# A two-layer transformer step on one core: the first weight unit of three stages taken in pieces

## The chip, the cores and the metric

The kernel runs on one core of a Trainium2 chip. The metric is the device time in microseconds of one execution. Three runs of the kernel before gave 1477.97, 1479.73 and 1479.81 us; the median is 1479.73 us.

## What is computed

One inference step for 384 tokens of width 1024: 128 prompt tokens and 256 sample tokens. Prompt and sample tokens have modulations of their own (shift, scale, gate, from `c_ctx` and `c`). All is float32.

```
for layer 0 and 1:
    h = x * (1 + scale) + shift            (modulate, per group of tokens)
    layer 0: q, k, v, p = h @ w_in_a ; differential attention and pooling ; @ w_out_a
    layer 1: h @ w_in_c ; two-way mLSTM over chunks ; @ w_out_c
    x = LayerNorm(alpha * x + gate * out)
    h = modulate(x)
    layer 0: SwiGLU with ffn_w_gu, ffn_w_down
    layer 1: router, top 2 of 8 experts, each a SwiGLU
    x = LayerNorm(alpha * x + gate * out)
```

The modulations come from `silu(c) @ ada_w + ada_b`, 12 vectors of 1024, so 12 x 4 MB of weights.

## The kernel before, in words

**Products.** Every dense weight comes in units of 128 x 1024 floats (512 KB) through a ring of six slots: `raw` (as loaded by SyncE, `stream`, L422 to L436), `whi` (ScalarE's copy in the rounded type, `Splits`, L453) and `wlo` (VectorE's remainder, raw minus whi, L456). The activations are held in the same two parts: `H32` is the modulated input, `Hh` its rounded copy, `Hl` the remainder. A product is three matmuls, whi x Hh, whi x Hl and wlo x Hh. `t_product` (L470 to L472) takes a unit of 128 output columns against all 384 tokens: for each of the eight chunks k of 128 channels three matmuls of 384 columns, so 24 matmuls. Its result goes to bank 6 or 7 of PSUM in turn; the semaphores free6 and free7 say when a reader has emptied the bank. Units of `ada_w` are not split; they go through the ring as `raw` and are multiplied with 32 columns of weights (L600).

**The start.** SyncE issues nine small loads (constants, masks, vectors), four units of `ada_w`, the three tiles of X, and then the stream. ScalarE waits for all nine (`cst_loaded`) before it makes the conditioning vectors. PE multiplies four ada units, waits for X, turns X with 24 transposes (L696), and goes on with ada units until the first two modulation vectors are there (`modc_made`; 16 units). With them ScalarE (L717) and VectorE (L729) make H32 out of PSUM, tile by tile of 128 tokens; ScalarE rounds (L745, L751), VectorE subtracts (L757, L760). `hl_made` counts finished tiles. `pe_mixer0` waits for all three and then takes, in the order of `INA_ORDER`, one t-unit of `w_in_a` and two ada units, eight times (they are called t0 to t7 here), and then units of the value part. GpSimd issues the loads of the caches and of the pooling matrices (2 MB) when the second modulation vector is there (`arow_made`).

**Between the stages.** Behind the output projection of layer 0 and behind its SwiGLU a norm follows, written out by hand for each engine (`dve_norm`, `act_norm`, `n_last`, `pe_turn`). They are called norm 0 and norm 1 here. VectorE scales tile t, PE turns it, ScalarE (and for half of the third tile VectorE) modulates it, ScalarE rounds, VectorE subtracts. `keep_clock` (L523) issues matmuls whose result nobody reads, 18 and then 12. When all of Hl is made (`hl_made`), GpSimd multiplies X with the norm's gain and adds its bias in six operations on 128 x 1024 (`pool_norm`, L849 and L850).

**Behind norm 0** `pe_ffn` waits for two tiles, but its first product reads all three and so stands behind the last piece of Hl. The order of units is g0, u0, g1, u1, d0, g2 and on (g and u are t-units, d is of the down projection). VectorE's order there is: split five units (L456), then multiply the first pair (L1227), which frees bank 7, then L1230. u1 writes bank 7, so it needs that first L1227. **Behind norm 1** `pe_mixer1` first makes the gates out of H32 (L1309, 16 matmuls), waits for `hl_made`, and takes 24 t-units m0 to m23. ScalarE copies each out (L1474); between the first and the second copy stands a step on the gates (L1413) that waits for a chain of VectorE (L1426 to L1429), which VectorE starts when it has split three units. m3 needs the bank of m1.

## Time and profile before

| what | value |
|---|---|
| median of three runs | 1479.73 us |
| the profiled execution, its own time | 1475.37 us |
| its span, first to last instruction | 1473.8 us |
| TensorE busy | 1388.6 us, 94% of the span |
| VectorE busy | 896.8 us, 61% |
| ScalarE busy | 725.5 us, 49% |
| GpSimd busy | 217.3 us, 15% |
| mean granted clock of TensorE | 0.979 of full |
| HBM read | 318.12 MB |

TensorE is busy nearly all the time, so a stage's length is mostly its matmuls; where TensorE stands still, the rest of the page says who ended the wait. The profiled execution took 4.4 us less than the median of the runs.

### The profile page before, as it was taken

How to read it: one execution, taken by the hardware profiler on the slowest of the kernel's cores; microseconds unless marked ns; L12 is line 12 of the kernel's file. 1: busy time of each engine (PE TensorE's matmuls, PEld its weight loads, DVE VectorE, ACT ScalarE, POOL GpSimd, SP SyncE). 2: the span in 40 equal slices, each digit the busy share in tenths (PEclk: the TensorE clock that was granted, in tenths of full speed). 3: DMA queues.
4: the chain of work that ended last, by engine and by line, in shares of the span. 5: the costliest groups of instructions: out<-in, count | busy, mean ns of one | idle time of the engine just before them, and what ended most of it. 6: DMA issues, size and time to landing. Idle time of an engine off the chain costs nothing.

```text
span 1473.8 us, 20822 instructions
## 1 busy us (share of the span) xinstructions
PE 1388.6 (94%) x6930; PEld 1142.7 (78%) x6930; DVE 896.8 (61%) x1187; ACT 725.5 (49%) x1125; POOL 217.3 (15%) x278
## 2 busy tenths in 40 slices
PE   6899888999999989999879899999999999999997
PEld 2766467999999979987557788888888888878784
DVE  0425557633333478222886597755555899999997
ACT  1323555232223353322443586445444888888883
POOL 1000001600000014003430372300000520000010
PEclk9999989999999999999999799999999999999998
DMA  9885563784444414537756499866765999999991
GB/s 326 280 266 204 200 197 111 280 288 129 129 129 129 129 43 127 147 113 232 247 195 215 143 345 381 288 186 187 227 187 181 326 383 378 383 372 380 377 364 58
DMA packets 255110, 341.23 MB, mean 232 GB/s; under 512 B 16910, under 2 KB 210732, under 8 KB 254908
## 3 DMA queue, kind: packets, MB, share of 16 engines
q1 hardware_dynamic: 241354, 299.55, 61.8%
q0 software_dynamic: 12400, 40.67, 7.4%
q8 instruction: 45, 0.74, 0.2%
q10 hardware_dynamic: 1282, 0.04, 0.0%
q14 instruction: 29, 0.24, 0.0%
HBM read 318.12 MB, written 21.02 MB: 230 GB/s over the span
## 4 chain that ended last, share of the span: by engine, by line
PE 82%; DVE 10%; ACT 3%; issue 2%; DMA 2%; SPq 1%; DVEq 0%; ACTq 0%
PE PS L2153 25%; PE PS L481 15%; PE PS L2160 12%; PE PS L470 6%; PE PS L471 6%; PE PS L472 6%; PE PS L600 2%; DVE wlo L456 2%; PE PS L2128 1%; PE PS L696 1%; PE PS L625 1%; DMA X<-in_x_sample 1%; DMA raw<-in_w_in_a 1%; DVE Hl L2026 1%; ACT BIG L1496 1%
## 5 line engine op out<-in xcount | busy, mean ns | idle before, releaser
L456 DVE TENSOR_TENSOR wlo<-raw,whi 128x1024 fp32r<-128x1024 f32 x130 | 172.1, 1352 | 227.6 <-ACT whi L453 227.2
L1958 DVE TENSOR_TENSOR wlo<-BIG,whi 128x1024 fp32r<-128x1024 f32 x192 | 239.5, 1262 | 71.1 <-ACT whi L1954 70.0
L1954 ACT ACTIVATE whi<-BIG 128x1024 fp32r<-128x1024 f32 x192 | 202.8, 1060 | 68.4 <-PE PS L2153 41.4
L2153 PE MATMUL PS<-whi,Hh 128*128 128x512 f32 x560 | 224.0, 400 | 2.3 <-DVE Hl L2026 2.2
L2153 PE MATMUL PS<-whi,Hl 128*128 128x512 f32 x560 | 219.8, 392 | 0.0
L2153 PE MATMUL PS<-wlo,Hh 128*128 128x512 f32 x560 | 219.5, 392 | 0.0
L470 PE MATMUL PS<-Hh,whi 128*128 128x384 f32 x608 | 206.3, 339 | 12.0 <-DVE Hl L760 8.1
L1958 DVE TENSOR_TENSOR wlo<-raw,whi 128x1024 fp32r<-128x1024 f32 x144 | 177.1, 1241 | 47.8 <-ACT whi L1954 46.5
L471 PE MATMUL PS<-Hl,whi 128*128 128x384 f32 x608 | 204.5, 336 | 0.0
L472 PE MATMUL PS<-Hh,wlo 128*128 128x384 f32 x608 | 204.4, 336 | 0.0
L1954 ACT ACTIVATE whi<-raw 128x1024 fp32r<-128x1024 f32 x144 | 152.2, 1059 | 57.3 <-PE PS L2160 30.4
L453 ACT ACTIVATE whi<-raw 128x1024 fp32r<-128x1024 f32 x130 | 133.6, 1052 | 81.3 <-DMA raw<-in_w_in_a 65.8
L470 PEld LDWEIGHTS PS<-Hh,whi 128*128 128x128 f32 x608 | 115.1, 189 | 20.0 <-DVE Hl L760 9.3
L2153 PEld LDWEIGHTS PS<-whi,Hh 128*128 128x128 f32 x560 | 105.6, 189 | 24.8 <-DVE Hl L2026 2.2
L2153 PEld LDWEIGHTS PS<-whi,Hl 128*128 128x128 f32 x560 | 105.5, 188 | 23.1
L2153 PEld LDWEIGHTS PS<-wlo,Hh 128*128 128x128 f32 x560 | 105.8, 189 | 20.9
L471 PEld LDWEIGHTS PS<-Hl,whi 128*128 128x128 f32 x608 | 115.2, 189 | 1.0 <-issue 0.2
L472 PEld LDWEIGHTS PS<-Hh,wlo 128*128 128x128 f32 x608 | 115.0, 189 | 0.0
L2160 PE MATMUL PS<-whi,gu_h 128*128 128x512 f32 x224 | 72.6, 405 | 2.1 <-DVE gu_l L2046 2.1
L2160 PE MATMUL PS<-whi,gu_l 128*128 128x512 f32 x224 | 70.4, 395 | 0.0
L2160 PE MATMUL PS<-wlo,gu_h 128*128 128x512 f32 x224 | 70.2, 394 | 0.0
L481 PE MATMUL PS<-whi,Hh 128*128 128x512 f32 x198 | 65.0, 410 | 4.8 <-DVE wlo L456 4.8
(384 smaller groups left out, 1948.4 us busy)
## 6 DMA issues: line engine op xcount, KB each, us to landing
raw<-in_moe_w_gu SPq DMA_DIRECT2D x224, 256.0 KB, 5.9
BIG<-in_moe_w_gu SPq DMA_DIRECT2D x224, 256.0 KB, 5.6
raw<-in_ada_w SPq DMA_DIRECT2D x96, 512.0 KB, 5.1
BIG<-in_moe_w_down SPq DMA_DIRECT2D x80, 512.0 KB, 8.0
raw<-in_ffn_w_gu SPq DMA_DIRECT2D x44, 512.0 KB, 4.8
raw<-in_w_in_c SPq DMA_DIRECT2D x32, 512.0 KB, 4.0
raw<-in_moe_w_down SPq DMA_DIRECT2D x32, 512.0 KB, 7.6
scr_tok<-BIG POOLq DMA_DIRECT2D x28, 512.0 KB, 10.0
```

Of the source, the lines that this page charges most:

```text
L453: self.eng.activation(whi[:, s, :], raw[:, s, :], ACT.Copy).then_inc(hi_made, 1)
L456: self.eng.tensor_tensor(wlo[:, s, :], raw[:, s, :], whi[:, s, :].bitcast(f32), ALU.subtract).then_inc(lo_made, 1)
L470: pe.matmul(PS[:, b, 0:T], wh, Hh[:, k, :], start=(k == 0), stop=False)
L471: pe.matmul(PS[:, b, 0:T], wh, Hl[:, k, :], start=False, stop=False)
L472: last = pe.matmul(PS[:, b, 0:T], wl, Hh[:, k, :], start=False, stop=(k == KT - 1))
L481: last = pe.matmul(PS[:, 2 * t + half, :], lhs, w[:, s, 512 * half:512 * half + 512], start=(first and lhs is h and w is whi), stop=(final ...
L600: last = pe.matmul(PS[at:at + 32, s.acc_bank(q), :], cw[:, k, :], raw[:, n % RING, 512 * half:512 * half + 512], start=(k < 2), stop=(k >= ...
L625: pe.matmul(PS[:, s.spread_bank(q), :], C("comb", 128, 2 * half + grp, 1).to_broadcast([128, 128]), arow, start=True, stop=True).then_inc( ...
L1954: act.activation(whi[:, slot(v), :], moe_raw(v), ACT.Copy).then_inc(hi_made, 1)
L1958: dve.tensor_tensor(wlo[:, slot(v), :], moe_raw(v), whi[:, slot(v), :].bitcast(f32), ALU.subtract).then_inc(lo_made, 1)
L2153: last = pe.matmul(PS[:, 6 * b + c % 2, :], lhs, wt[:, s, 512 * k:512 * k + 512], start=(q == 0 and k == 0 and lhs is h and wt is whi), st ...
L2160: last = pe.matmul(PS[:, 2 + 2 * b + half, :], lhs, wt[:, s, 512 * half:512 * half + 512], start=(c == 0 and q == 0 and lhs is h and wt is ...
```

## The change

Five edits.

1. SyncE issues the first two ada units behind two of the nine small loads instead of behind all nine.
2. GpSimd issues the 2 MB of caches and pooling matrices when PE has used the first t-unit, not when the second modulation vector is there.
3. The first H is made by chunks of channels, not by tiles of tokens. The transposes write the banks so that both sample tiles of a chunk lie side by side, and one operation takes 256 columns of them. ScalarE makes chunks 0 to 3 and VectorE 4 to 7; rounding and subtraction go in three cuts (chunks 0 and 1, 2 to 4, 5 to 7). The first t-unit waits for one cut at a time.
4. Behind norms 0 and 1 the first t-unit runs for tokens 0 to 255 when two tiles are ready, and then for the third tile in 24 matmuls of 128 columns. Behind norm 1 the gates stand between the two. ScalarE and VectorE finish the second tile ahead of the third.
5. The second `keep_clock` behind these norms issues 6 instead of 12.

```diff
+            if n == U_INA_T:
+                for i, cut in enumerate(FIRST_CUTS):
+                    pe.wait_ge(hl_made, i + 1)
+                    last = t_part(pe, b, s, 0, T, *cut)
+            else:
+                last = t_part(pe, b, s, 0, T)
+            last.then_inc(unit_used, 1)
+
+        def t_part(pe, b, s, lo, hi, first=0, end=KT):
+
+            for k in range(first, end):
...
+                pe.matmul(PS[:, b, lo:hi], wh, Hh[:, k, lo:hi], start=(k == 0), stop=False)
+                pe.matmul(PS[:, b, lo:hi], wh, Hl[:, k, lo:hi], start=False, stop=False)
+                last = pe.matmul(PS[:, b, lo:hi], wl, Hh[:, k, lo:hi], start=False, stop=(k == KT - 1))
+            return last
+
+        def t_two_tiles(pe, st, n, w):
...
+            pe.wait_ge(hl_made, TT * st + TT - 1)
+            t_part(pe, b, n % RING, 0, 256)
+
+        def t_third_tile(pe, st, n, w):
+
+            pe.wait_ge(hl_made, TT * st + TT)
+            t_part(pe, b67(w)[0], n % RING, 256, T).then_inc(unit_used, 1)
...
             if st < 2:
-                keep_clock(pe, 12)
+                keep_clock(pe, 6)
...
+        FIRST_CUTS = ((0, 2), (2, 5), (5, KT))
+
+        def first_mod(eng, half, op):
+
+            eng.wait_ge(modc_made, 1)
+            eng.wait_ge(turned, 2 * TT)
+            for c in range(4):
+                i = 4 * half + c
+                op(H32[:, i, 0:128], PS[:, half, 128 * c:128 * c + 128], modc[:, 1, i, 1:2], modc[:, 0, i, 1:2])
+                last = op(H32[:, i, 128:T].rearrange("p (a n) -> p a n", a=2),
+                          PS[:, 2 + 2 * half:4 + 2 * half, 128 * c:128 * c + 128], modc[:, 1, i, 0:1], modc[:, 0, i, 0:1])
+            return last
...
+            dve.wait_ge(h32_act, TT)
+            dve.wait_ge(h32_dve, TT)
+            for i, (lo, hi) in enumerate(FIRST_CUTS):
+                dve.wait_ge(hh_made, 2 * i + 2)
+                dve.tensor_tensor(Hl[:, lo:hi, :], H32[:, lo:hi, :], Hh[:, lo:hi, :].bitcast(f32), ALU.subtract
+                                  ).then_inc(hl_made, 1)
...
             if parts:
                 dve_lower(dve, st + 1, 0, 2)
+                dve_lower(dve, st + 1, 1, 4)
             dve_mod(dve, st + 1, TT - 1)
             if parts:
-                dve_lower(dve, st + 1, 2, 3, 0)
-                dve_lower(dve, st + 1, 1, 5)
+                dve_lower(dve, st + 1, 2, 5, 0)
                 dve_lower(dve, st + 1, 2, 6, 1)
...
+                act_mod(act, st + 1, 1, (0, 1))
+                act_rstd(act, ch, st, 2)
+                act_upper(act, st + 1, 1)
+                act_mod(act, st + 1, 2, (0,))
+                act_upper(act, st + 1, 2, 0)
+                act_upper(act, st + 1, 2, 1)
+                return
...
+            t_two_tiles(pe, 2, U_INC_T, W_INC)
             wait_h32(pe, 2, TT - 1)
...
-            pe.wait_ge(hl_made, 3 * TT)
-            for m in range(24):
+            t_third_tile(pe, 2, U_INC_T, W_INC)
+            for m in range(1, 24):
...
+            stream(sp, 0, 2)
...
-            stream(sp, 0, 4)
+            stream(sp, 2, 4)
...
-            pool.wait_ge(arow_made, FIRST[1])
+            pool.wait_ge(unit_used, U_INA_T + 1)
```

What this moves, at three places. First SyncE at the start (`BIG` here is the room of the small vectors). Before:

```order
L2353 DMA BIG<-in_c 8x128
L2354 DMA BIG<-in_c_ctx 8x128
L2355 DMA BIG<-in_pool_scale 4x128
L2356 DMA BIG<-in_mlstm_norm_g 8x128
L2357 DMA BIG<-in_diff_norm_g 1x128
L2359 DMA BIG<-in_ln_g 32x128
L2359 DMA BIG<-in_ln_b 32x128
L2361 DMA cst<-in_const 128x929
L2362 DMA BIG<-in_masks 128x256
L436 DMA raw<-in_ada_w 128x1024 x4
```

and now:

```order
L2412 DMA BIG<-in_c 8x128
L2413 DMA BIG<-in_c_ctx 8x128
L436 DMA raw<-in_ada_w 128x1024 x2
L2415 DMA BIG<-in_pool_scale 4x128
L2416 DMA BIG<-in_mlstm_norm_g 8x128
L2417 DMA BIG<-in_diff_norm_g 1x128
L2419 DMA BIG<-in_ln_g 32x128
L2419 DMA BIG<-in_ln_b 32x128
L2421 DMA cst<-in_const 128x929
L2422 DMA BIG<-in_masks 128x256
L436 DMA raw<-in_ada_w 128x1024 x2
```

Two units of 512 KB now stand ahead of the constants for which ScalarE waits.

Second VectorE behind norm 0, from the scaling of the third tile on (`128x8x128` is the Hl of one tile, `128x4x128` half a tile). Before:

```order
L783 TENSOR_SCALAR X<-X,mv,rstd 128x1024 [waits rstd_made]
L757 TENSOR_TENSOR Hl<-BIG,Hh 128x8x128 [waits hh_made,h32_act]
L729 TENSOR_SCALAR BIG<-PS,modc 128x128 [waits turned,modc_made]
L729 TENSOR_SCALAR BIG<-PS,modc 128x128 x3
L760 TENSOR_TENSOR Hl<-BIG,Hh 128x4x128 [waits hh_made,h32_dve,h32_act]
L757 TENSOR_TENSOR Hl<-BIG,Hh 128x8x128 [waits hh_made,h32_act]
L760 TENSOR_TENSOR Hl<-BIG,Hh 128x4x128 [waits hh_made,h32_dve,h32_act]
L456 TENSOR_TENSOR wlo<-raw,whi 128x1024 [waits hi_made] x5
L1227 TENSOR_TENSOR BIG<-BIG,PS 128x384 [waits free6,unit_used]
```

and now:

```order
L839 TENSOR_SCALAR X<-X,mv,rstd 128x1024 [waits rstd_made]
L813 TENSOR_TENSOR Hl<-BIG,Hh 128x8x128 [waits hh_made,h32_act] x2
L753 TENSOR_SCALAR BIG<-PS,modc 128x128 [waits turned,modc_made]
L753 TENSOR_SCALAR BIG<-PS,modc 128x128 x3
L816 TENSOR_TENSOR Hl<-BIG,Hh 128x4x128 [waits hh_made,h32_dve,h32_act] x2
L456 TENSOR_TENSOR wlo<-raw,whi 128x1024 [waits hi_made] x5
L1285 TENSOR_TENSOR BIG<-BIG,PS 128x384 [waits free6,unit_used]
```

The second tile's subtraction now stands ahead of the third tile's modulation. The five splits and the multiplication behind them keep their places.

Third TensorE behind norm 1 (L1309 and L1368 are the gates). Before:

```order
L523 MATMUL PS<-cr 128x384 x12
L1309 MATMUL PS<-BIG 64x384 [waits wg_cut,h32_dve,h32_act]
L1309 MATMUL PS<-BIG 64x384 x7
L470 MATMUL PS<-Hh,whi 128x384 [waits lo_made,free6,hl_made]
L471 MATMUL PS<-Hl,whi 128x384
```

and now (of the first 24 matmuls the first and the last, of the second 24 the first two):

```order
L546 MATMUL PS<-cr 128x384 x6
L480 MATMUL PS<-Hh,whi 128x256 [waits hl_made,lo_made,free6]
...
L482 MATMUL PS<-Hh,wlo 128x256
L1368 MATMUL PS<-BIG 64x384 [waits wg_cut,h32_dve,h32_act]
L1368 MATMUL PS<-BIG 64x384 x7
L480 MATMUL PS<-Hh,whi 128x128 [waits hl_made]
L481 MATMUL PS<-Hl,whi 128x128
```

The gates, which stood behind 12 spare matmuls, now stand behind 6 and behind the first 24 of the unit.

## Rows read from the trace of the kernel before

**Rows 1.** The page, its chain that ended last, shares by engine

```profile
PE 82%; DVE 10%; ACT 3%; issue 2%; DMA 2%; SPq 1%; DVEq 0%; ACTq 0%
```

**Rows 2.** Windows: stretch, length, busy by engine (count), TensorE clock, DMA share, GB/s

```profile
0.00:5.60 5.60, 0.00 (x0) 0.00 (x0) 0.00 (x0) 1.21 (x1) 2.22 (x8) 1.00 0.30 35
...
46.60:53.00 6.40, 6.40 (x33) 5.31 (x32) 0.45 (x1) 1.05 (x2) 0.00 (x0) 0.79 0.31 100
53.00:80.00 27.00, 27.00 (x161) 21.56 (x162) 5.50 (x5) 5.85 (x9) 1.03 (x2) 1.00 0.89 272
```

**Rows 3.** Timeline, SyncE's queue: start us, length us, engine, line, operation

```profile
1.77 0.29 SPq L2355 DMA_DIRECT2D BIG<-in_pool_scale  x1
...
4.56 1.88 SPq L436 DMA_DIRECT2D raw<-in_ada_w  x4
```

**Rows 4.** Chain that ended last, 0 to 80 us: start us, us, what

```profile
7.55 10.13 DMA X<-in_x_sample
```

**Rows 5.** Timeline, all engines, from the second modulation vector on

```profile
36.90 0.17 DVE L658 TENSOR_SCALAR modc<-PS 128x16 f32<-128x16 f32 x1 [1.15 <-PE PS L618]
...
37.17 2.90 ACT L717 ACTIVATE BIG<-PS,modc 128x128 f32<-128x128 f32 x8 [0.39 <-DVEq L667]
...
38.36 3.91 DVE L729 TENSOR_SCALAR BIG<-PS,modc 128x128 f32<-128x128 f32 x12
...
39.92 1.10 ACT L745 ACTIVATE Hh<-BIG 128x1024 fp32r<-128x1024 f32 x1
...
42.19 2.52 DVE L757 TENSOR_TENSOR Hl<-BIG,Hh 128x1024 fp32r<-128x1024 f32 x2
...
45.97 0.69 PE L470 MATMUL PS<-Hh,whi 128*128 128x384 f32 x1 [5.42 <-DVE Hl L760]
...
51.85 1.06 PE L600 MATMUL PS<-raw,cw 128*32 128x512 f32 x8
```

**Rows 6.** Windows of the first t-unit, columns as in rows 2

```profile
46.00:47.00 1.00, 1.00 (x3) 1.00 (x4) 1.00 (x1) 0.00 (x0) 0.00 (x0) 0.50 1.01 420
```

**Rows 7.** DMA issues: count, KB each, us to landing (issued in 50:56, then 38:38.6)

```profile
raw<-in_w_in_a SPq DMA_DIRECT2D x1, 512.0 KB, 6.0
...
raw<-in_w_in_a SPq DMA_DIRECT2D x1, 512.0 KB, 11.7
```

**Rows 8.** Timeline, TensorE, the ada units ahead of t3

```profile
62.62 1.06 PE L600 MATMUL PS<-raw,cw 128*32 128x512 f32 x8
```

**Rows 9.** Timeline behind norm 0, all engines

```profile
245.34 1.09 PE L696 MATMUL PS<-cst,X 128*128 128x128 f32 x8 [1.52 <-DVE X L783]
...
249.63 3.88 ACT L453 ACTIVATE whi<-raw 128x1024 fp32r<-128x1024 f32 x4
250.45 0.69 DVE L760 TENSOR_TENSOR Hl<-BIG,Hh 128x512 fp32r<-128x512 f32 x1
...
251.19 0.69 PE L470 MATMUL PS<-Hh,whi 128*128 128x384 f32 x1 [2.65 <-DVE Hl L760]
251.29 3.22 POOL L849 TENSOR_TENSOR X<-X,BIG 128x1024 f32<-128x1024 f32 x1 [33.73 <-DVE Hl L760]
```

**Rows 10.** Timeline, VectorE and TensorE, from the second split on

```profile
252.19 3.41 DVE L456 TENSOR_TENSOR wlo<-raw,whi 128x1024 fp32r<-128x1024 f32 x1
...
265.55 0.54 DVE L1227 TENSOR_TENSOR BIG<-BIG,PS 128x384 f32<-128x384 f32 x1
...
266.15 0.44 PE L470 MATMUL PS<-Hh,whi 128*128 128x384 f32 x1 [0.88 <-DVE BIG L1227]
```

**Rows 11.** Timeline behind norm 1, TensorE, VectorE and GpSimd

```profile
544.81 2.80 PE L1309 MATMUL PS<-BIG 128*64 128x384 f32 x16
...
547.39 1.22 DVE L456 TENSOR_TENSOR wlo<-raw,whi 128x1024 fp32r<-128x1024 f32 x1
...
547.63 3.25 POOL L849 TENSOR_TENSOR X<-X,BIG 128x1024 f32<-128x1024 f32 x1 [232.58 <-DVE Hl L760]
...
562.08 0.45 PE L470 MATMUL PS<-Hh,whi 128*128 128x384 f32 x1 [1.79 <-ACT BIG L1474]
```

More of the change, by code:

```diff
@@ L467, in t_product @@
             pe.wait_ge(lo_made, split_count(n))
-            for k in range(KT):
-                wh, wl = whi[:, s, 128 * k:128 * k + 128], wlo[:, s, 128 * k:128 * k + 128]
-                pe.matmul(PS[:, b, 0:T], wh, Hh[:, k, :], start=(k == 0), stop=False)
-                pe.matmul(PS[:, b, 0:T], wh, Hl[:, k, :], start=False, stop=False)
-                last = pe.matmul(PS[:, b, 0:T], wl, Hh[:, k, :], start=False, stop=(k == KT - 1))
-            last.then_inc(unit_used, 1)
+            if n == U_INA_T:
[7 more added lines that the diff above has]
+            for k in range(first, end):
+                wh, wl = whi[:, s, 128 * k:128 * k + 128], wlo[:, s, 128 * k:128 * k + 128]
+                pe.matmul(PS[:, b, lo:hi], wh, Hh[:, k, lo:hi], start=(k == 0), stop=False)
[3 more added lines that the diff above has]
+        def t_two_tiles(pe, st, n, w):
+            b, freed, before = b67(w)
+            pe.wait_ge(freed, before)
+            pe.wait_ge(lo_made, split_count(n))
+            pe.wait_ge(hl_made, TT * st + TT - 1)
[3 more added lines that the diff above has]
+            t_part(pe, b67(w)[0], n % RING, 256, T).then_inc(unit_used, 1)
         def n_tile(pe, n, t, sh, sl, first, final):
@@ L695, in pe_turn @@
             for i in range(KT):
-                last = pe.transpose(PS[:, 2 * t + i // 4, 128 * (i % 4):128 * (i % 4) + 128],
+                bank = 2 * t + i // 4 if st or t == 0 else 1 + t + 2 * (i // 4)
+                last = pe.transpose(PS[:, bank, 128 * (i % 4):128 * (i % 4) + 128],
                                     X[:, t, 128 * i:128 * i + 128], C("ident"))
@@ L732, in dve_mod, with act_first, dve_first @@
             last.then_inc(h32_dve, 1)
+        FIRST_CUTS = ((0, 2), (2, 5), (5, KT))
[8 more added lines that the diff above has]
+            return last
+        def act_first(act):
+            first_mod(act, 0, lambda out, x, scale, shift: act.activation(out, x, ACT.Identity, bias=shift, scale=scale)
+                      ).then_inc(h32_act, TT)
+            act.wait_ge(h32_act, TT)
+            for i, (lo, hi) in enumerate(FIRST_CUTS):
+                if i == 1:
+                    act.wait_ge(h32_dve, TT)
+                act.activation(Hh[:, lo:hi, :], H32[:, lo:hi, :], ACT.Copy).then_inc(hh_made, 2)
+        def dve_first(dve):
+            first_mod(dve, 1, lambda out, x, scale, shift: dve.tensor_scalar(out, x, scale, shift, ALU.mult, ALU.add)
+                      ).then_inc(h32_dve, TT)
+            dve.wait_ge(h32_act, TT)
+            dve.wait_ge(h32_dve, TT)
+            for i, (lo, hi) in enumerate(FIRST_CUTS):
+                dve.wait_ge(hh_made, 2 * i + 2)
+                dve.tensor_tensor(Hl[:, lo:hi, :], H32[:, lo:hi, :], Hh[:, lo:hi, :].bitcast(f32), ALU.subtract
+                                  ).then_inc(hl_made, 1)
         def wait_h32(eng, st, t):
@@ L815, in act_norm @@
                 act_upper(act, st + 1, 0)
+            if parts:
+                act_mod(act, st + 1, 1, (0, 1))
[5 more added lines that the diff above has]
+                return
             act_mod(act, st + 1, 1, (0,))
@@ L818, in act_norm @@
             act_mod(act, st + 1, 1, (1,))
-            if not parts:
-                act_hn(act, 0)
+            act_hn(act, 0)
             act_mod(act, st + 1, 2, (0,))
-            if parts:
-                act_upper(act, st + 1, 2, 0)
-                act_upper(act, st + 1, 1)
-                act_upper(act, st + 1, 2, 1)
-            else:
-                act_hn(act, 1)
-                act_hn(act, 2)
+            act_hn(act, 1)
+            act_hn(act, 2)
         def log_exp(act):
@@ L940, in pe_mixer0 @@
         def pe_mixer0(pe):
-            pe.wait_ge(hl_made, TT)
             ada = Ada(pe, "pe", None, MID)
@@ L1189, in pe_ffn @@
         def pe_ffn(pe):
-            pe.wait_ge(hl_made, 2 * TT)
             pe.wait_ge(modc_read, cols_before(EARLY[1]))
-            for kind, c in FFN_ORDER[:-FFN_LAST]:
+            t_two_tiles(pe, 1, U_FFN, W_FFN)
+            t_third_tile(pe, 1, U_FFN, W_FFN)
+            for kind, c in FFN_ORDER[1:-FFN_LAST]:
                 n = FFN_AT[kind, c]
@@ L2402, in _ @@
             sp_.upto(U_INA_T)
-            act_mod(act, 0, 0, (0,))
-            act_mod(act, 0, 1, (0,))
-            act_upper(act, 0, 0)
-            act_mod(act, 0, 2, (0,))
-            act_upper(act, 0, 1)
-            act_upper(act, 0, 2, 0)
-            act_upper(act, 0, 2, 1)
+            act_first(act)
             act_mixer0(act, ch, sp_)
@@ L2436, in _ @@
             sp_.upto(U_INA_T)
-            for t in range(TT):
-                dve_mod(dve, 0, t)
-            dve_lower(dve, 0, 0, 2)
-            dve_lower(dve, 0, 1, 4)
-            dve_lower(dve, 0, 2, 5, 0)
-            dve_lower(dve, 0, 2, 6, 1)
+            dve_first(dve)
             dve.wait_ge(lam_step, 5)
```

## The prediction

> **What bounds the kernel now.** I read the page first, then the chain of waits, then the timeline at the three places that the change touches, and the DMA view beside them. The chain runs through TensorE for 82% of the span and through VectorE for 10% [rows 1]: only stretches in which TensorE stands still, or waits for VectorE, can give anything. Near the change there are five.
>
> At the start DMA bounds: up to 5.6 us the queues move 35 GB/s [rows 2], since the first large load comes fourth from the end of the small ones and the weights are issued only at 4.56 [rows 3]. The chain waits 10.13 us for X, which lands at 17.7 [rows 4]. Then the modulation is ready at 37.07 and TensorE starts t0 at 45.97, after 5.42 us of standing still; t0 ends at 51.85 [rows 5], so it takes 5.9 us. Behind norm 1 three t-units lie between the end of the gates (544.81 + 2.80) and the stop at 562.08 - 1.79 = 560.29 [rows 11]: 4.2 us each, or 0.175 us per matmul. So t0 loses 1.7 us to the low clock: the granted clock at 46 to 47 us is 0.50 [rows 6], the 1.2 GHz level.
>
> Behind norm 0 TensorE stands still for 2.65 us ahead of g0 [rows 9]. That looks like the prize, but it stops again ahead of u1, 0.88 us, for VectorE's multiplication L1227, at 266.15 [rows 10]. VectorE comes there late because its splits take 3.41 us each [rows 10] where they take 1.22 without GpSimd [rows 11]. Behind norm 1 the gates fill the wait, and TensorE stops ahead of m3, for 1.79 us, for ScalarE's copy, which stands behind the same kind of VectorE chain [rows 11].
>
> **Part 1, earlier loads.** The first two ada units go out at 1.77 instead of 4.56 [rows 3]. Data of large loads began to flow at 5.6 [rows 2], about 2 us after the first of them was issued (the constants, one place ahead of the masks and the weights), so now at about 3.8: a gain of at most 1.8 us. It is at least nothing: the constants now lie behind 1 MB, 2.5 us at 400 GB/s, and ScalarE waits for them. X is issued at the same time as before and profits only from what has been moved ahead of it. I take 1.2 us, two thirds, since TensorE also comes to the transposes after a longer rest.
>
> **Part 2, the first unit.** ScalarE's 128-column modulation costs 2.90/8 = 0.36 us, VectorE's 3.91/12 = 0.33 [rows 5]. Per 128 more columns ScalarE needs 0.12 (1.10 less its fixed part for 1024) and VectorE 0.15 (1.26 for 1024) [rows 5]. Four small and four wide ones: ScalarE 3.4 us, from 37.17 to 40.6; VectorE 3.2, from 38.36 to 41.6. Then ScalarE rounds cut 1 (768 columns, 0.85 us, at 41.45), VectorE subtracts it (0.95) until 42.6; the other cuts take 1.2 and 1.4 us each, so VectorE is done at 44.3 and 45.7. TensorE starts at 42.7 and has nine matmuls left at 45.75: 1.6 us at the full clock, 2.9 at half. t0 ends at 47.4 to 48.7 instead of 51.85, a gain of 3.2 to 4.5. TensorE's rest shrinks from 5.42 us to about 2.1, below the 2.65 behind which the clock was low, so I take 4.0.
>
> **Part 3, GpSimd's 2 MB moved.** Before, they ran while TensorE waited. Now they start when t0 is used, into a stretch that was idle (DMA share 0.31 from 46.6 to 53) but goes to 0.89 [rows 2]. The nearest consumer is t3. Its unit is issued right behind the ada units used at 52.9 [rows 5], so at 53.8, lands 6.0 us later [rows 7], is split in 1.06 + 1.22, and is ready at 62.2; TensorE wants it at 62.62 + 1.06 = 63.7 [rows 8]. The cover is 1.5 us. A unit of the same kind, issued at 38.5 with the 2 MB in the air, landed after 11.7 us [rows 7]. That bounds the stall above: 11.7 - 6.0 - 1.5 = 4.2 us; below it is nothing. At 400 GB/s 2.1 MB are 5 us, of which some 1.7 run before the stream starts; 3.3 less the cover is 1.8 us, which I take. The caches are needed only at the units of the value part, tens of us later, so nobody else waits. The bias load behind them on GpSimd is needed after eight ada units, also later. SyncE is not moved past anything there.
>
> **Part 4, behind norm 0.** VectorE's subtraction takes 1.26 us [rows 5] and begins with the transposes at about 245.2 [rows 9]; two in a row end at 247.7, and g0 starts there, 3.5 us earlier. Its 24 matmuls of 256 columns take two thirds of 4.2, 2.8 us. The third tile has no row of its kind: between a third (1.4 us) and the price of 384 columns (4.2). The nearest row is the transposes, also 128 columns, 1.09/8 = 0.136 us each [rows 9], so 3.3. g0 ends at 253.8, and TensorE comes to u1 at 262.2 instead of 265.3. But u1 waits for L1227, and that stands behind five splits. The chain of VectorE begins with the last piece of Hl, which ends at 250.45 + 0.69 = 251.14 [rows 9] and now at about 250.4 (247.7, third tile's modulation 1.3, then the last rounding and subtraction, 1.4 together). ScalarE's first rounded weight, begun at 249.63 [rows 9], can come only 0.1 earlier, so the first split starts at 250.6 instead of 251.05. That is all that is gained: 0.45 us. TensorE now stands still for 3.5 us ahead of u1, longer than the 2.65 behind which the clock was at half for g0 (g0 and the two units behind it took 266.15 - 0.88 - 251.19 = 14.1 us, 1.5 more than three times 4.2). Before, those 1.5 us were hidden by the stop ahead of u1; now they fall behind it, on the path. Norm 0 in sum: 1.05 us lost.
>
> **Part 5, behind norm 1.** The two tiles start at about 544.4, then the gates (2.8), the third tile (3.3) and two units: 561.7 (with 4.2 for either piece it would be 564), against a release that was at 562.08 and comes 0.15 earlier, with VectorE. Gain 0.15. The six spare matmuls cost nothing: their place ends just where the first tiles are ready; if these came later, TensorE would rest there.
>
> **Sum.** 1.2 + 4.0 - 1.8 - 1.05 + 0.15 = 2.5 us gained. The profiled execution, 1475.37 us, would be 1472.9; it lies 4.4 under the median of the runs, 1479.73, so the median goes to 1477.2. What is not bounded by TensorE behind these places moves with it, since every ring slot is freed by TensorE or VectorE.
>
> **Rival A, slower: GpSimd comes first.** Before, VectorE's first split began at 251.05, GpSimd's operation at 251.29 [rows 9], and again 547.39 and 547.63 [rows 11]. Each time that first split took 1.22 and those behind it 3.41: VectorE and GpSimd take turns, GpSimd's share being 3.35 - 1.2 = 2.15 us. Now GpSimd is let go at 250.4 + 0.15 = 250.55 and the first split at 250.6: a tie. If GpSimd is first, the split ends at 253.9 instead of 252.3, L1227 comes 1.6 us later, and with the clock norm 0 loses 3.1; behind norm 1 the same costs 1.9. Sum: 3.4 - 3.1 - 1.9 = -1.6, 1481.3 us, and up to 1485 with a full stall at t3 and a second fall of the clock. It decides by who starts first; 0.1 us turns it. The Trainium skill, "SBUF — State Buffer", Terms, says of the port that these two share that it is exclusive and held for the whole instruction, so that "the loser fully blocks"; by that rule, with which the 3.41 us agree, it is a matter of order and not of bandwidth.
>
> **Rival B: t3 stalls in full.** If both queues get equal turns on the DMA engines, t3 waits 4.2 us, and the clock falls, 1.5 more: 5.2 - 5.7 - 0.9 = -1.4, 1481.1 us. For it speaks the 11.7 us; against it, that this unit had more ahead of it in its own queue. The Trainium skill, "DMA: Bandwidth & Descriptors", Queues, rings and completion order, says that each DMA engine goes round robin between its queues by packets; the trace before doesn't show the turns.
>
> **Rival C: no stall at t3** and t0 wholly at the full clock: 5.7 - 0.9 = 4.8, 1474.9 us.
>
> **Rival D: TensorE's earlier start behind norm 0 is kept** (VectorE's splits are no bound): 3.1 gained there instead of 1.05 lost, 1473.1 us. Against it speaks the 0.88 us stop.
>
> **Numbers.** Forecast 0.34, A 0.26, B 0.12, C 0.18, D 0.10. A measurement of this kernel tells about 0.2%, 3 us. Faster by more: most of C, all of D, the upper end of the forecast: 0.34. Slower by more: the lower halves of A and B: 0.18. The rest, 0.48, is the same. Range 1473.0 to 1483.0: from D to the middle of A's and B's own ranges.
>
> **What would show it.** Right: t0 done near 46 to 47 us; a wait for t3 of 1 to 3 us; behind norm 0 g0 starts with no rest, and a rest of 3 us or more ahead of u1; the first split 1.2 us long both times. A first split of over 3 us shows A; no rest ahead of u1 shows D. It would be wrong if X landed no earlier, or if the pieces of 128 columns cost over 4 us.

## The result, and the profile after

The kernel with the change takes 1485.15 us, the median of 7 runs (1483.12 to 1487.84); beside it the kernel before took 1478.12 (7 runs, 1474.55 to 1479.81). The ratio is 1.0049, with a 95% interval of 1.0035 to 1.0063: 7 us slower. The forecast was 1477.2, in a range of 1473.0 to 1483.0.

The page of the profile after (engine by engine: busy us, share of the span, instructions; then the shares of the chain that ended last):

```profile
span 1483.5 us, 20876 instructions
...
PE 1393.4 (94%) x6966; PEld 1149.0 (77%) x6966; DVE 896.6 (60%) x1182; ACT 724.8 (49%) x1120; POOL 216.6 (15%) x278
...
PE 52%; DVE 7%; ACT 2%; issue 2%; DVEq 0%; ACTq 0%
```

The span grew by 9.7 us in these two executions (1473.8 before). TensorE is busy 4.8 us more, and that is not the 36 more matmuls alone (48 of narrower pieces and 12 fewer spare ones): part of it is the same work at a lower granted clock. The chain here adds up to 63%: its reconstruction ends in the middle of the program, so unlike [rows 1] it doesn't reach the places that matter. I therefore went along the program and asked at marked instructions how much later they start than before. Here is where that offset changes.

**The first unit.** Windows of the start (stretch, length, busy by engine, clock, DMA share, GB/s), then the timeline (start us, length us, engine, line, operation):

```profile
0.00:5.60 5.60, 0.00 (x0) 0.00 (x0) 0.00 (x0) 1.08 (x1) 2.22 (x8) 1.00 0.42 127
46.00:47.00 1.00, 1.00 (x8) 1.00 (x7) 0.56 (x1) 0.00 (x0) 0.00 (x0) 1.00 0.00 0
```

```profile
1.78 0.83 SPq L436 DMA_DIRECT2D raw<-in_ada_w  x2
```

```profile
10.38 0.31 ACT L2449 ACTIVATE BIG<-BIG 16x128 f32<-16x128 f32 x1 [4.58 <-DMA BIG<-in_masks]
```

```profile
36.88 0.17 DVE L681 TENSOR_SCALAR modc<-PS 128x16 f32<-128x16 f32 x1 [1.15 <-PE PS L641]
...
37.11 4.96 PE L546 MATMUL PS<-cr 128*128 128x384 f32 x18 [0.27 <-DVE modc L681]
37.15 3.33 ACT L772 ACTIVATE BIG<-PS,modc 128x128 f32<-128x128 f32 x8 [0.41 <-DVEq L690]
...
38.34 3.17 DVE L781 TENSOR_SCALAR BIG<-PS,modc 128x128 f32<-128x128 f32 x8
...
42.70 0.41 PE L480 MATMUL PS<-Hh,whi 128*128 128x384 f32 x1 [0.64 <-DVE Hl L787]
```

```profile
47.56 1.06 PE L623 MATMUL PS<-raw,cw 128*32 128x512 f32 x8
```

The weights go out at 1.78 and 127 GB/s flow where 35 did [rows 2], but ScalarE waits for the last of the constants until 10.38, and the second modulation vector is ready at 36.88, before at 36.90 [rows 5]: in this pair of executions the earlier loads brought nothing. The chunks did: t0 starts at 42.70 and ends at 47.56, before at 45.97 and 51.85 [rows 5], with the clock at 1.00 where it was 0.50 [rows 6]. 4.3 us are gained. The low clock has not gone, it comes earlier: the 18 spare matmuls ahead of t0, whose result nobody reads, take 4.96 us (3.42 before), with the granted clock at 0.50 from 39 to 41 us, and from 42 us on it is 1.00 again.

**The stop ahead of t3.** The transfers issued from 48 to 51 us (count, KB each, us to landing), then TensorE and ScalarE, then windows:

```profile
BIG<-in_poolm POOLq DMA_DIRECT2D x1, 1280.0 KB, 10.5
raw<-in_ada_w SPq DMA_DIRECT2D x2, 512.0 KB, 5.2
raw<-in_w_in_a SPq DMA_DIRECT2D x1, 512.0 KB, 12.2
```

```profile
61.74 1.06 ACT L453 ACTIVATE whi<-raw 128x1024 fp32r<-128x1024 f32 x1 [8.20 <-DMA raw<-in_w_in_a]
...
64.20 0.66 PE L480 MATMUL PS<-Hh,whi 128*128 128x384 f32 x1 [4.80 <-DVE wlo L456]
```

```profile
49.00:50.00 1.00, 1.00 (x7) 1.00 (x7) 0.87 (x1) 0.10 (x1) 1.00 (x2) 1.00 0.54 123
```

```profile
64.00:68.00 4.00, 3.80 (x12) 3.83 (x13) 0.86 (x2) 1.06 (x1) 0.00 (x0) 0.50 1.08 366
68.00:72.00 4.00, 4.00 (x23) 2.91 (x22) 0.41 (x1) 1.16 (x2) 0.00 (x0) 0.88 0.20 52
```

The unit of t3, issued at 49.50, lands after 12.2 us (6.0 before [rows 7]), and TensorE stands still for 4.80 us. Behind it the granted clock is 0.50, the lower of its two levels (1.2 GHz): 12 matmuls start in the first of these windows, 23 in the second. The next stop of the program starts at 84.93 - 1.31 = 83.62 us, before at 82.15 - 1.25 = 80.90: 4.3 gained have become 2.7 lost, 7.0 us in this one place. From there to the transposes of norm 0 the offset grows to 5.0, but that tells more of the trace before than of the change: from the end of that stop to TensorE's last transposes ahead of norm 0 it took 163.2 us, the change takes 165.4, and the other twelve kernels below take 164.7 to 168.8, 164.7 in one whose code up to there is that of the kernel before.

**Behind norm 0** (all engines; TensorE's row at 252.72 is a matmul of 256 columns):

```profile
250.36 1.09 PE L720 MATMUL PS<-cst,X 128*128 128x128 f32 x8 [1.55 <-DVE X L839]
```

```profile
252.72 0.36 PE L480 MATMUL PS<-Hh,whi 128*128 128x256 f32 x1 [0.21 <-DVE Hl L813]
```

```profile
255.58 14.53 DVE L456 TENSOR_TENSOR wlo<-raw,whi 128x1024 fp32r<-128x1024 f32 x5 [0.16 <-ACT whi L453]
270.03 0.54 DVE L1285 TENSOR_TENSOR BIG<-BIG,PS 128x384 f32<-128x384 f32 x1
```

```profile
255.58 3.48 POOL L907 TENSOR_TENSOR X<-X,BIG 128x1024 f32<-128x1024 f32 x1 [33.00 <-DVE Hl L816]
```

```profile
270.62 0.69 PE L480 MATMUL PS<-Hh,whi 128*128 128x384 f32 x1 [3.80 <-DVE BIG L1285]
```

```profile
270.00:272.00 2.00, 1.38 (x4) 1.38 (x5) 1.34 (x3) 1.40 (x3) 2.00 (x1) 0.59 0.27 79
272.00:274.00 2.00, 2.00 (x8) 2.00 (x8) 2.00 (x2) 1.40 (x3) 1.92 (x2) 0.55 0.63 188
```

TensorE starts on the two tiles after 0.21 us of standing still (2.65 before [rows 9]), but it stands still for 3.80 us ahead of u1 (0.88 before [rows 10]), and now the low clock falls behind that stop. VectorE and GpSimd start in the same hundredth of a microsecond.

**Behind norm 1:**

```profile
550.27 0.35 PE L480 MATMUL PS<-Hh,whi 128*128 128x256 f32 x1 [0.20 <-DVE Hl L813]
```

```profile
553.12 2.38 POOL L907 TENSOR_TENSOR X<-X,BIG 128x1024 f32<-128x1024 f32 x1 [232.61 <-DVE Hl L816]
```

```profile
553.13 10.12 DVE L456 TENSOR_TENSOR wlo<-raw,whi 128x1024 fp32r<-128x1024 f32 x3 [0.16 <-ACT whi L453]
```

```profile
570.01 0.44 PE L480 MATMUL PS<-Hh,whi 128*128 128x384 f32 x1 [2.70 <-ACT BIG L1533]
```

Here GpSimd is 0.01 us ahead, its operation takes 2.38 us as if undisturbed, and VectorE's three splits take 10.12 us in place of 7.91 (before, 547.39 to 555.30; [rows 11] has the first of them): 2.2 us more. The stop ahead of m3 is 2.70 us (1.79 [rows 11]).

### The profile page after: what moved, and what is told of

It is laid out like the page before. It is cut to its first block, busy times and chain, and to the rows that moved or that the text cites. A ratio compares the mean times of both kernels' runs of the same rounds, so it can differ in the third digit from the quotient of the medians.

```text
span 1483.5 us, 20876 instructions
## 1 busy us (share of the span) xinstructions
PE 1393.4 (94%) x6966; PEld 1149.0 (77%) x6966; DVE 896.6 (60%) x1182; ACT 724.8 (49%) x1120; POOL 216.6 (15%) x278
## 4 chain that ended last, share of the span: by engine, by line
PE 52%; DVE 7%; ACT 2%; issue 2%; DVEq 0%; ACTq 0%
PE PS L2212 25%; PE PS L2219 12%; PE PS L504 5%; PE PS L480 2%; PE PS L481 2%; PE PS L482 2%; PE PS L2187 1%; DVE wlo L456 1%; ACT BIG L1555 1%; DVE Hl L2085 1%; PE PS L2257 0%; DVE BIG L1615 0%; PE PS L1775 0%; ACT whi L2013 0%; PE PS L1799 0%
## 5 line engine op out<-in xcount | busy, mean ns | idle before, releaser
L480 PE MATMUL PS<-Hh,whi 128*128 128x384 f32 (+1 forms) x624 | 210.9, 338 | 13.9 <-DVE wlo L456 6.1
L481 PE MATMUL PS<-Hl,whi 128*128 128x384 f32 (+1 forms) x624 | 209.2, 335 | 0.0
L482 PE MATMUL PS<-Hh,wlo 128*128 128x384 f32 (+1 forms) x624 | 208.9, 335 | 0.0
L480 PEld LDWEIGHTS PS<-Hh,whi 128*128 128x128 f32 x624 | 119.0, 191 | 22.4 <-issue 13.9
L481 PEld LDWEIGHTS PS<-Hl,whi 128*128 128x128 f32 x624 | 118.9, 191 | 1.0 <-issue 0.2
L482 PEld LDWEIGHTS PS<-Hh,wlo 128*128 128x128 f32 x624 | 118.9, 191 | 0.0
```

Source lines behind the costliest of these rows:

```text
L480: pe.matmul(PS[:, b, lo:hi], wh, Hh[:, k, lo:hi], start=(k == 0), stop=False)
L481: pe.matmul(PS[:, b, lo:hi], wh, Hl[:, k, lo:hi], start=False, stop=False)
L482: last = pe.matmul(PS[:, b, lo:hi], wl, Hh[:, k, lo:hi], start=False, stop=(k == KT - 1))
```

## The experiments

**Which part costs what.** Four kernels, each timed in 5 rounds beside the kernel before. In the expectations "part 1" to "part 5" are the five edits of the change in their order (the prediction numbers its parts otherwise). The edits against the change, or against the kernel before:

```diff
# pool_loads_back, against the change
-            pool.wait_ge(unit_used, U_INA_T + 1)
+            pool.wait_ge(arow_made, FIRST[1])
# loads_and_pool_back, the same and
-            stream(sp, 0, 2)
-            stream(sp, 2, 4)
+            stream(sp, 0, 4)
# norms_back, against the change
-            t_two_tiles(pe, 1, U_FFN, W_FFN)
-            t_third_tile(pe, 1, U_FFN, W_FFN)
-            for kind, c in FFN_ORDER[1:-FFN_LAST]:
+            pe.wait_ge(hl_made, 2 * TT)
+            for kind, c in FFN_ORDER[:-FFN_LAST]:
...
-                keep_clock(pe, 6)
+                keep_clock(pe, 12)
```

> The change with one part undone: GpSimd issues its 2 MB again when the first two modulation vectors are made. Theory S (the moved 2 MB hold back the unit of t3, and TensorE's clock is low behind that stop): no wait ahead of t3, clock 1.00 from 62 to 70 us, and the kernel comes back by 4.8 + 2.5 = 7.3 us, to 0.3 below the kernel before. Rival R1 (the 2 MB were moved because early they hold back the units of t1 and t2, which are now wanted 4.3 us earlier): a stop of 2 to 4 us ahead of t1 or t2 takes the place of the stop ahead of t3, and the kernel stays 3 to 5 us above the one before. Rival R2 (the loss comes from the norms, the 24 added matmuls and the fewer spare ones): 2 us or less come back.

> The change with parts 4 and 5 undone: behind both norms all three tiles go into the first unit at once, ScalarE's and VectorE's order is the old one, 12 spare matmuls. Theory S prices these parts from the trace at 0.9 us lost behind norm 0 and 2.7 behind norm 1: 3.6 come back, the kernel is 3.4 above the one before. Rival R2 (the norms carry most of the loss): 5 to 7 us come back. Rival R3 (they carry nothing, the offsets are of other causes): 1 us or less.

> The change with the 2 MB and the first two ada units both issued at their old places. Theory S: the start is bound by the DMA engines whatever their order, so this is equal to the kernel with only the 2 MB put back, within 1 us, and the second modulation vector is ready at 36.9 in both. Rival R4 (my forecast's part 1: the earlier ada units are worth 1.2 us, lost in the trace of the change by something else): this is 1.2 us slower than the kernel with only the 2 MB put back.

> The kernel before with part 3 of the change alone (the first unit by chunks). Theory S: the 4.3 us gained at t0 are kept to the end, 1473.8 against 1478.1. Rival R1: t1 or t2 waits for its unit, 1 to 2 us of gain are left. Rival R5 (any earlier arrival is taken back by a later stop that is bound by DMA or VectorE): within 1 us of the kernel before.

Measured: pool_loads_back 1477.65 us, ratio to the kernel before 1.0001 (0.9992 to 1.0010); norms_back 1479.54, 1.0009 (1.0000 to 1.0019); loads_and_pool_back 1478.14, 1.0009 (1.0000 to 1.0018); first_unit_alone (the kernel before with edit 3 only) 1474.16, 0.9971 (0.9961 to 0.9981).

So the moved 2 MB cost 0.0048 of the time, 7.1 us, as theory S said: with them back there is no stop ahead of t3, and none ahead of t1 or t2 either, though the unit of t2 lands after 11.4 us there:

```profile
raw<-in_w_in_a SPq DMA_DIRECT2D x1, 512.0 KB, 11.4
```

R1 falls: issued at 37.06 us in that trace, the unit has time. The first unit alone keeps its whole gain, 4.3 us. The norms cost 1.0009 - 0.9971 = 0.0038, 5.6 us (4.0 by the medians), and taken out of the change they give back as much: 1.0049 - 1.0009 = 0.0040, 5.9 us. That is the 5 to 7 of rival R2, though the 2 MB carry still more, and not the 3.6 that I had read from one trace. The earlier loads can't be told from nothing by the times (1.0001 against 1.0009, 1.2 us apart, intervals that overlap), so neither theory S nor R4 falls by them. In the traces the second modulation vector starts at 35.9 us on average in the seven kernels with the earlier loads (34.95 to 36.88), and at 36.8 in the seven without (35.97 to 37.60): some 0.9 us, near R4's 1.2.

**The 2 MB without the rest of the change.** The kernel before, with one line:

```diff
-            pool.wait_ge(arow_made, FIRST[1])
+            pool.wait_ge(unit_used, U_INA_T + 1)
```

> The kernel before with part 2 of the change alone: GpSimd's 2 MB wait until t0 is used. Theory S: POOL issues them at about 52, the unit of t3 follows at 53.8, shares the DMA engines with them, and TensorE stops ahead of t3 for 4 to 5 us, with the clock low behind it: 5.5 to 7.5 us slower than the kernel before, 1484 to 1486. Rival R10 (the stop ahead of t3 comes only with the first unit's earlier end): stop below 2 us, at most 2 us slower.

Measured: 1485.10 us, ratio 1.0046 (1.0033 to 1.0058), +6.8 us. TensorE's stop, and the landing of the unit:

```profile
70.14 0.66 PE L470 MATMUL PS<-Hh,whi 128*128 128x384 f32 x1 [4.91 <-DVE wlo L456]
```

```profile
raw<-in_w_in_a SPq DMA_DIRECT2D x1, 512.0 KB, 12.3
```

R10 falls: the stop has nothing to do with the first unit's earlier end. One line of the change, put into the kernel before, loses as much as the whole change; in the rest of it the gain of the first unit and of the loads (4.3 and some 0.9) and the loss at the norms (5.6) cancel each other.

**GpSimd's start behind the norms.** In the traces above the new norms came out in two ways. In pool_loads_back VectorE was first behind norm 1, and the stop ahead of m3 was 0.46 us; in loads_and_pool_back, the same code there, GpSimd was first and the stop was 2.69:

```profile
544.10 3.46 POOL L907 TENSOR_TENSOR X<-X,BIG 128x1024 f32<-128x1024 f32 x1 [232.62 <-DVE Hl L816]
```

```profile
544.75 2.38 POOL L907 TENSOR_TENSOR X<-X,BIG 128x1024 f32<-128x1024 f32 x1 [232.62 <-DVE Hl L816]
```

The next kernels have the change with the 2 MB back (first_gpsimd_after_splits: the kernel before with edit 3) and an extra wait ahead of GpSimd's operations, or spare matmuls ahead of u1:

```diff
                 pool.wait_ge(hl_made, TT * (st + 2))
+                pool.wait_ge(lo_made, split_count((U_FFN + 2, U_INC_T + 3)[st]))           # after_one_split
+                pool.wait_ge(lo_made, split_count((U_FFN + RING, U_INC_T + RING)[st]))     # after_splits
# spare_before_u1
+                    if n == U_FFN + 3:
+                        wait_h32(pe, 1, TT - 1)
+                        keep_clock(pe, 16, 0)
```

> The change with the 2 MB put back, and behind each norm GpSimd starts only when VectorE's first split there has ended, so VectorE is always first. Theory T (behind norm 1 both are let go within 0.01 us and whoever comes first takes the port: with GpSimd first the stop ahead of m3 was 2.70 us, with VectorE first 0.46): the first split takes 1.2 us behind both norms, the stop ahead of m3 is below 0.6 us, that ahead of u1 stays at 3.8, and the kernel gains up to 2.2 us, 1 to 2 in the median, over the one with only the 2 MB put back (1477.65). Rival R6 (who is first follows from something else, such as ScalarE's copy): the stop ahead of m3 stays at 2.7.

> The change with the 2 MB put back, and GpSimd's operations behind each norm start when the ring's splits there have been made (five behind norm 0, four behind norm 1), so that VectorE has the port alone. Theory T (VectorE's splits at 3.41 us in place of 1.22 are what holds up u1 and m3, and absorb what the two-tile start gains): splits 1.22 us each, the first multiplication behind norm 0 starts 8.5 us earlier, no stop ahead of u1 and m3, no low clock there; against the one with only the 2 MB put back 3.8 + 1.5 us are gained at norm 0 and 0.5 to 2.7 at norm 1, 5 to 7 in all, so 1471 to 1473. Rival R7 (the six operations of GpSimd, 19 us, collide later with VectorE's next splits just as much): the stops only move, gain below 2 us.

> The kernel before with the first unit by chunks, and GpSimd's operations behind each norm start when the ring's splits there have been made; the norms otherwise as before (three tiles at once). Theory T: the stops ahead of u1 (0.6) and m3 (1.8) go, so that 2.4 us are gained over the first unit alone (1474.2), to 1471.8; against the same kernel with two tiles first it is slower by what two tiles first are worth without contention: 2.65 + 1.5 of stop and clock less 1.35 for the third tile (2.85 + 2.7 - 4.2), 2.8 us. Rival R8 (two tiles first are worth nothing even so, as the 24 added matmuls and the chain of VectorE cost what it gains): both within 1 us.

> The change with the 2 MB put back, and 16 spare matmuls of 384 columns (3.0 us at the full clock) ahead of u1, in the stop of 3.8 us. Theory C (TensorE's standing still is what lowers the granted clock behind u1, at 1.5 us): the clock stays 1.00 from u1 on, the stop left is below 1 us, and 1.5 us are gained over the one with only the 2 MB put back, 1476.2. Rival R9 (the clock behind u1 is low for another reason, as the two low-clock stretches of the attention part are): still 0.50 behind u1, nothing gained.

Measured: after one split 1468.89, ratio 0.9944 (0.9930 to 0.9957); after the splits 1469.57, 0.9942 (0.9927 to 0.9957); the first unit with GpSimd after the splits 1470.04, 0.9951 (0.9935 to 0.9967); spare matmuls 1476.41, 0.9985 (0.9970 to 1.0001).

A wait that lets GpSimd start one split later gains 0.0057, 8 us, where I expected 1 to 2. The trace says why: GpSimd starts 0.2 us after the second split has started, so two splits run free and not one; the five take 12.38 us and not 14.53, and the stop ahead of u1 shrinks to 1.65 us, behind which the clock stays at 1.00:

```profile
248.33 12.38 DVE L456 TENSOR_TENSOR wlo<-raw,whi 128x1024 fp32r<-128x1024 f32 x5 [0.16 <-ACT whi L453]
260.63 0.54 DVE L1286 TENSOR_TENSOR BIG<-BIG,PS 128x384 f32<-128x384 f32 x1
```

```profile
261.23 0.44 PE L480 MATMUL PS<-Hh,whi 128*128 128x384 f32 x1 [1.65 <-DVE BIG L1286]
```

My expectation that the stop ahead of u1 stays at 3.8 was wrong, and with it the size; the first split was 1.2 us long as theory T said, and R6 fell: the stop ahead of m3 is gone. In the table below this kernel is 4.7 us shorter behind norm 0 than the one with only the 2 MB back, and 2.3 behind norm 1 (VectorE had been first there in that trace, and the clock fell once more than here).

With GpSimd after the splits there is no stop ahead of u1 or m3, and 1469.57 is below the 1471 to 1473 of theory T; R7 falls. The pair that should tell what two tiles first are worth without contention missed its forecast of 2.8 us: 1469.57 against 1470.04, within the 1 us of rival R8. In the traces the stretch is 3.7 us shorter with the new norms behind norm 0 and 2.1 longer behind norm 1, where the clock fell twice in the one and once in the other (see under the table). The execution with the new norms also lost 2.5 us at t0, where the clock fell behind a rest of 1.64 us:

```profile
42.76 0.41 PE L480 MATMUL PS<-Hh,whi 128*128 128x384 f32 x1 [1.64 <-DVE Hl L787]
```

```profile
44.00:48.00 4.00, 3.79 (x13) 3.73 (x13) 2.62 (x3) 0.82 (x1) 0.00 (x0) 0.57 0.89 319
```

The spare matmuls tell what the clock costs. The windows of the stop and behind it, first without them (pool_loads_back), then with them:

```profile
260.00:262.00 2.00, 0.00 (x0) 0.00 (x0) 1.96 (x2) 0.01 (x1) 2.00 (x2) 0.71 0.65 196
262.00:264.00 2.00, 1.99 (x6) 1.99 (x7) 1.38 (x1) 2.00 (x4) 1.92 (x2) 0.50 0.59 177
264.00:266.00 2.00, 2.00 (x7) 2.00 (x7) 2.00 (x2) 0.78 (x1) 2.00 (x1) 0.50 0.28 85
```

```profile
262.00:264.00 2.00, 2.00 (x13) 2.00 (x13) 1.61 (x2) 2.00 (x4) 1.92 (x2) 1.00 0.73 219
264.00:266.00 2.00, 2.00 (x13) 2.00 (x13) 2.00 (x1) 0.56 (x1) 2.00 (x1) 1.00 0.15 44
```

Six or seven matmuls in 2 us without, thirteen with, and the time is 1477.65 against 1476.41 (by the ratios 2.4 us). The stop left is 1.09 us. R9 falls in the trace; the timed intervals overlap, so the size rests on single traces: by the table below the stretch behind norm 0 is 2.5 and 2.7 us shorter than in the two kernels with the 2 MB back, and 1.4 shorter than in the change.

**The best of each.** Three kernels with GpSimd held back for five splits behind norm 0 and for one behind norm 1: `(U_FFN + RING, U_INC_T + 3)[st]` in the line above.

> The change with the 2 MB put back; GpSimd starts behind norm 0 after five splits, behind norm 1 after one. Each was the better choice at its norm in the traces of the two runs before (from the first Hl of the norm on: 4.6 gained at norm 0 with five, 2.7 with one; at norm 1 the kernel with one was 3.7 better than that with four). Theory T: no stop ahead of u1 or m3, and 1 to 3 us below the better of the two (1468.9), 1466 to 1468. Rival R11 (the difference at norm 1 was one of executions, not of the wait): 1469 to 1470.

> The kernel before with the first unit by chunks and GpSimd's waits as in the kernel beside it (five splits, then one), the norms otherwise as before. Theory T: without contention two tiles first are worth 2 to 3 us, so this is 1468 to 1471, slower than the kernel beside it by that much. Rival R8 (two tiles first are worth nothing even so): within 1 us of it.

> The kernel before with nothing but GpSimd's waits (five splits behind norm 0, one behind norm 1). Theory T: the stops of 0.88 us ahead of u1 and 1.79 ahead of m3 go, 2.7 us and some low clock behind them: 1475 to 1476, the first split 1.2 us in both. Rival R7 (GpSimd's operations collide later with VectorE as much): within 1 us of the kernel before.

Measured: gpsimd_mix 1466.52, ratio 0.9918 (0.9904 to 0.9932); first_gpsimd_mix 1469.87, 0.9947 (0.9929 to 0.9965); before_gpsimd_mix 1474.88, 0.9977 (0.9966 to 0.9988). The first is 11.3 us faster than the kernel before, the fastest here: the change with one line undone and one added. R11 falls by the times, though the intervals of the ratios just touch (0.9904 to 0.9932 against 0.9930 to 0.9957 for GpSimd after one split). The first two differ by 0.0029, 4.3 us (3.4 by the medians), by two tiles first and by the earlier loads, which only the first has. So without contention two tiles first are worth some 3 us in this pair, 3.7 behind norm 0 and 1.0 behind norm 1 in the traces, and R8 falls here, narrowly; in the pair before they had been worth the same 3.7 behind norm 0, and almost nothing in the times. With contention they cost 5.6 by the ratios, 4.0 by the medians. In before_gpsimd_mix R7 falls, and 1474.88 is where theory T had it, but the gain is behind norm 1 (2.6 us in the traces, one fall of the clock less among it) and not behind norm 0, where the low clock lasted longer in that trace. VectorE and GpSimd behind norm 0 in gpsimd_mix:

```profile
247.81 4.63 DVE L456 TENSOR_TENSOR wlo<-raw,whi 128x1024 fp32r<-128x1024 f32 x4 [0.15 <-ACT whi L453]
253.41 1.23 DVE L456 TENSOR_TENSOR wlo<-raw,whi 128x1024 fp32r<-128x1024 f32 x1 [0.97 <-ACT whi L453]
254.93 0.56 DVE L1286 TENSOR_TENSOR BIG<-BIG,PS 128x384 f32<-128x384 f32 x1 [0.30 <-PE PS L482]
```

```profile
254.81 2.41 POOL L908 TENSOR_TENSOR X<-X,BIG 128x1024 f32<-128x1024 f32 x1 [40.02 <-DVE wlo L456]
```

VectorE waits there for TensorE, and not the other way round. Later splits do meet GpSimd (6.77 us for the next two), but TensorE then has work ahead of it.

The stretches behind the norms, worked out from each trace. Norm 0: from TensorE's last transposes (250.36 above) to VectorE's sixth multiplication of the feed-forward part (326.76 in the change). Norm 1: from the last transposes (547.91) to VectorE's 128x3 operation L1631 (703.09).

| kernel | norms | norm 0, us | norm 1, us |
|---|---|---|---|
| before | old | 75.48 | 150.91 |
| first unit alone | old | 75.49 | 152.51 |
| norms back | old | 75.49 | 152.70 |
| 2 MB moved alone | old | 75.49 | 151.87 |
| the change | new | 76.40 | 155.18 (GpSimd first) |
| 2 MB back | new | 77.53 | 151.28 (VectorE first) |
| 2 MB and loads back | new | 77.73 | 155.10 (GpSimd first) |
| spare matmuls ahead of u1 | new | 75.02 | 155.15 (GpSimd first) |
| GpSimd after one split | new | 72.79 | 148.97 |
| GpSimd after the splits | new | 70.86 | 152.66 |
| first unit, after the splits | old | 74.57 | 150.57 |
| mix | new | 70.85 | 149.63 |
| first unit, mix | old | 74.59 | 150.58 |
| before, mix | old | 75.78 | 148.29 |

One row is one execution, and in the column of norm 1 the clock makes differences that the edits don't. Further on in that stretch all fourteen traces have two more stops, of 1.6 us near 650 and of 2.2 near 690; the clock is low behind the first in eight of them and behind the second in seven, behind both in three (norms back; GpSimd after the splits; first unit, mix) and behind neither in two (GpSimd after one split; before, mix), which are the two shortest. Each such fall makes some 1.6 us, so differences of that size, or of twice that between no fall and two, say nothing. What holds: new norms under contention cost 0.9 to 2.2 us behind norm 0, and 3.1 behind norm 1 when GpSimd is first (155.1 against the mean of 152.0 of the four old ones without an added wait, 150.9 to 152.7).

## Why the prediction was wrong

Two steps of the sum failed: part 3, which took 1.8 us for the moved 2 MB where they cost 7, and part 5, which took 0.15 gained behind norm 1 where the change loses 3.1 once GpSimd is first there. With part 4 the norms were to cost 0.9 us and cost 5.6.

**Part 1, earlier loads (1.2 gained): neither confirmed nor refuted.** The rate at the start rose as forecast, but in this trace the constants came 2.8 us later (ScalarE at 10.38, 7.62 before), and the modulation ended at the same time. X did land earlier (TensorE starts on it at 16.89 us; it landed at 17.68 before [rows 4]), which I had named as the sign of the gain, and in this trace it was worth nothing, since TensorE then stood still for 1.73 us, up to 27.22, for the next weights. The fourteen traces together show some 0.9 us.

**Part 2, the first unit (4.0 gained): right**, 4.3 in the trace, 4.3 by the ratio of the kernel with it alone, and by the steps given: ScalarE 3.33 for 3.4, VectorE 3.17 for 3.2, TensorE at 42.70 for 42.7. With the clock it had luck. I had TensorE rest for 2.1 us ahead of t0; in ten of the eleven traces that have the new first unit the clock fell earlier, on the spare matmuls, where it cost nothing, and the rest was 0.6 to 0.7 us in nine of them. In the eleventh (gpsimd_mix) it stayed at 1.00 throughout, with a rest of 2.20 us. In gpsimd_after_splits it fell a second time, behind a rest of 1.64 us, and t0 ended 13.2 us after the start of the second modulation vector, 10.7 in the others.

**Part 3, the 2 MB (1.8 lost): the first step that failed.** It cost 7 us. Of the 5 us of traffic the sum took off too much ("some 1.7 run before the stream starts"), and it left the clock out. There was no start ahead: GpSimd's first load was issued at 47.92, the units at 48.65 to 49.50, but the DMA engines moved nothing before 49 us and 123 GB/s in the microsecond from 49, and the largest load, 1.28 MB, was issued at 50.23, behind the unit of t3. So all 5 us of that traffic, and a share of the next pair of weights issued at 54, came in while the unit was under way: a landing of 12.2 us in place of 6.0. The upper bound that I had worked out, 4.2 us from a landing of 11.7 of a unit with the same 2 MB in the air [rows 7], was the measurement of just this case, and I argued it away with "this unit had more ahead of it in its own queue". The stop was 4.80. The Trainium skill, "DMA: Bandwidth & Descriptors", Queues, rings and completion order, says that the DMA engines go round robin between queues by packets; by that rule a load issued later on the other queue takes its turns from the unit at once, and the landing after 12.2 us agrees. The low clock behind the stop makes the rest: 7.0 us of offset less 4.8 is 2.2. That is rival B, with both its terms, at a chance of 0.12. With the 2 MB put back stop and low clock go (7.1 us), and moved alone they bring both (6.8 us).

**Part 4, behind norm 0 (1.05 lost): right** in the mechanism, and low by half in two of three traces: the rest ahead of u1 was 3.80 for 3.5, the clock fell behind it, the loss 0.9 in this trace. In the two kernels with the same code there it was 2.0 and 2.2, with the low clock from about 261 to 268 us; with the stop filled it is 0.5 gained (75.02 against 75.49). The third tile costs less than I took: six matmuls of 128 columns are 0.67 us apart, so 2.7 us, where I had 3.3 from the transposes; two tiles took 2.85 for 2.8. None of that could show, since VectorE was the bound.

**Part 5, behind norm 1 (0.15 gained): the second step that failed.** It took VectorE's splits there as before, and rival A came true. I had called the start of VectorE and GpSimd a tie that 0.1 us turns. It is one, to 0.01 us. Before, VectorE went from its last subtraction straight into the split and was 0.24 us ahead both times [rows 9, 11]; now it waits 0.16 us there for ScalarE's rounded weight, and that is the lead. In the four traces of the new order without an added wait VectorE came first behind norm 0 each time, and GpSimd behind norm 1 in three. The added wait that puts VectorE first behind norm 1 takes the stop away. The price, 2.15 us for the turn, was right (2.2 in the splits, 2.24 in the stop). The low clock behind the stop ahead of m3 (0.72 on average from 570 to 576) I had named only as an extreme. The rule of the Trainium skill that went with rival A ("SBUF — State Buffer", Terms: the port is held for the whole instruction, "the loser fully blocks") agrees with 10.12, 7.91 and 5.67 us (this last with GpSimd after one split) for the same three splits, with none, one and two of them free.

**The sum.** With what was measured: 0.9 + 4.3 - 7.0 - 5.6 (norms, by the ratios) is 7.4 lost, against 7 measured. A and B were priced as alternatives, 1481.3 and 1481.1. They have nothing to do with each other, and both happened. Rival A's text even has the sum of the two, 1485, but the range ends at 1483.0: it took them one at a time.

**What stays open.** The size of the norms' loss: 5.6 and 5.9 us by the ratios, 4.0 by the medians of the first of these pairs, 4.0 to 5.3 by the stretches in the traces. The worth of part 1 between nothing and 1.2 us. What two tiles first are worth behind norm 1 without contention (2.1 lost in one pair of traces, 1.0 gained in the other, each time with one fall of the clock more in the longer one). Why the clock falls behind one stop and not behind another of the same length, even at the same place of the program.

## What to carry to other kernels

An engine that starts earlier gains nothing when the one it waits for next sets the pace: first take away what slows that one (here GpSimd's operations beside VectorE's, by one wait), then the earlier start pays some 3 us (3.7 behind norm 0) in place of costing 4 to 5.6. When a transfer is moved, find a landing in the trace with the same bytes in the air and take that, and add the low clock to the stop (in the fourteen traces the clock was low behind every stop of 3.78 us and more. The length alone doesn't tell for shorter ones: behind the stop of 2.65 us at norm 0 it was always low, behind one of 3.21 near 770 us, which thirteen of them have, in nine and full in four, and behind stops of 1.6 to 2.2 us it came out either way). Independent risks add up: the range must hold the case in which two of them happen.
